# One hybrid decoder layer: output projection and down product turned so that features lie on partitions, the second norm moved behind the MLP

## The chip, the core and the metric

The kernel runs on one core of one Trainium2 chip. A core has TensorE (matmuls of a stationary 128x128 tile with a moving tile of up to 512 columns, into PSUM), VectorE, ScalarE, GpSimd and SP, whose queue issues the DMAs. The metric is device time in microseconds of one execution; lower is better. In the profile TensorE is PE, VectorE is DVE, ScalarE is ACT and GpSimd is POOL.

## The reference

One layer (DEPTH 1) on x of 1024 tokens by 1024 features, all in float32:

```python
merged = gates[:, :, 0] * y_attn + gates[:, :, 1] * y_pool
x = x + jnp.einsum('bsd,de->bse', merged, w_o[l])

h2 = rms_norm(x, norm2_g[l])
u = jnp.square(jax.nn.relu(jnp.einsum('bsd,df->bsf', h2, w_mlp_in[l])))
x = x + jnp.einsum('bsf,fd->bsd', u, w_mlp_out[l])
```

The attention and pooling branches ahead of `merged` are the same in both kernels. The row norm divides each token by the root of its mean square (plus 1e-6) and multiplies each feature by a gain. Since relu squared is homogeneous of second degree, a positive factor r of a token can be left out ahead of the up product and put in as r squared behind the down product.

## The kernel before

**Precision.** Each float32 operand is split into a rounded part (`_hi`, made by ScalarE) and the rest (`_lo`, a subtraction on VectorE, since `_lo = source - _hi`). A product of two such pairs is three matmuls (`passes`): hi by hi, lo by hi (or hi by lo), hi by lo.

**Output projection.** Eight token tiles in the order `ORDER`, two column halves each: 16 PSUM tiles of 128 tokens by 512 features, 24 matmuls each, with the merged activations stationary and `w_o` moving. VectorE adds the residual (`add_res`), SP stores the sum to `res_store`, ScalarE squares and sums the row, GpSimd takes its inverse root, VectorE multiplies by it and by the gain (`h2_norm`), and TensorE turns the row back with eight 128x128 transposes (`h2_transpose`). From the transposed tile ScalarE and VectorE make the hi and lo parts of seven left sides.

**MLP.** Both MLP products go by Winograd's form of Strassen's scheme: 7 products in place of 8. The up product has 16 pairs (`p`) of 256 hidden features; each pair has 7 products P5, P4, P1, P6, P2, P7, P3 of 12 matmuls with 512 columns. Per pair, VectorE makes four sums of the next pair's weights (`t_sums`), five lo parts, four sums of the last results (`u_sums`), three sums out of PSUM (`up_add`), two more lo parts, four more sums; ScalarE rounds, takes relu and square. A PSUM bank is used again by the product eight places on, so the second product of a pair (P4) waits for the sum that frees P5 of the pair before (the third of the last four). The weights come as one 1 MB load per pair into `pair_raw`. Squared activations go to `u_store` in DRAM and come back as `s_raw`.

The down product has 28 products (`n`), 4 chunks of 7, of four tiles with 12 matmuls each. VectorE splits product n+2 while it adds the tiles of n into `acc`, which is first loaded with the residual. In the last chunk GpSimd folds the sums that several quadrants share (`folded`). SP stores most of the output during the last product, and its four tiles (one of them in two halves) as they are done.

**Order.** All queues are written out by hand, each instruction with the semaphores it waits for. What decides the times around the change is the order on VectorE, which the diff shows in full for the projection.

Of the kernel before, what the change touches and what calls it, by code (L numbers as in the profile page):

```python
# [24 lines left out]
F32 = mybir.dt.float32  # L25
# [9 lines left out]
def trunk_layer(nc, x, norm1_g, w_in, b_gate, q_norm_g, k_norm_g, lam_params, subln_g,  # L35
# [26 lines left out]
    y_rows = y.rearrange("b (t p) d -> (b t) p d", p=P)  # L62
# [8 lines left out]
    with ExitStack() as ctx:  # L71
# [79 lines left out]
        ORDER = (4, 0, 5, 1, 6, 2, 7, 3)  # L151
# [4 lines left out]
        res = [at(f"res{i}", kb, [P, D]) for i, kb in enumerate((208, 212, 200))]  # L156
        g2_row = at("g2_row", 144, [P, D])
        a21_f = at("a21_f", 148, [P, QK, P])
        s1_f = at("s1_f", 150, [P, QK, P])
        h2_row = at("h2_row", 152, [P, D])  # L160
        s2_f = at("s2_f", 156, [P, QK, P])
        s34_f = at("s34_f", 158, [P, QK, P])
# [4 lines left out]
        pair_raw = [at(f"pair_raw{i}", 192 + 8 * i, [P, KD, 2 * P]) for i in range(2)]  # L167
# [7 lines left out]
        acc = at("acc", 0, [P, T, D])  # L175
# [18 lines left out]
        res_store = nc.dram_tensor("res_store", [T, P, D], F32, kind="Internal").ap()  # L194
# [13 lines left out]
        N_ROWS = 2 * D // P + GROUPS + 3  # L208
# [4 lines left out]
        small = at("small", 220.25, [P, 128])  # L213
        BG, PS, SG, QG, KG = 0, 2 * D // P, 2 * D // P + GROUPS, 2 * D // P + GROUPS + 1, 2 * D // P + GROUPS + 2
# [26 lines left out]
        def sem(name):  # L241
# [53 lines left out]
        (m_hi, m_split, wo_full, res_ready, r_squared, r_mean, r_inv, h2_ready, h2T_full, h2_hi, h2_f,  # L295
         h2_lo) = (sem(n) for n in (
             "m_hi", "m_split", "wo_full", "res_ready", "r_squared", "r_mean", "r_inv", "h2_ready", "h2T_full",
             "h2_hi", "h2_f", "h2_lo"))
# [3 lines left out]
        o_f, d_hi, d_lo, d_tile, d_added, v_moved, folded, y_ready = (sem(n) for n in (  # L302
            "o_f", "d_hi", "d_lo", "d_tile", "d_added", "v_moved", "folded", "y_ready"))
# [217 lines left out]
        def count_hi(s):  # L521

            return 8 * (s // 2) + 3 * (s % 2)

        def count_f(s):

            return 4 * (s // 2) + s % 2

        def count_lo(s):

            return 7 * (s // 2) + 2 * (s % 2)
# [3 lines left out]

        def b_quarter(p, q):

            return pair_raw[p % 2][(slice(None),) + QUARTER[q]]

        def wo_leaves(eng, p, i):  # L540

            left = i // 2 + 1
            if left == 4:
                eng.wait_ge(wo_full, 2 * T - 1 + p)
            else:
                eng.wait_ge(wo_left, 3 * p + left)
# [2231 lines left out]
```

## Time and profile before

| | |
|---|---|
| time, median of 3 runs | 1241.32 us (1241.32 to 1242.48) |
| profiled execution | 1241.36 us, span 1239.5 us |
| TensorE busy | 1228.6 us, 99% of the span |
| VectorE busy | 945.4 us, 76% |
| ScalarE busy | 563.9 us, 45% |
| GpSimd busy | 139.2 us, 11% |
| granted TensorE clock | 1.00 in every stretch |
| DMA | 173.95 MB, 140 GB/s mean |

The span is the time from the first to the last recorded instruction; the profiled execution's own time holds 1.9 us more. Busy TensorE is the union of matmul intervals, which overlap: a matmul of 512 columns is recorded with 389 ns, but the next starts 227 ns after it. In a timeline a row is `start us, us, engine line instruction out<-in xcount`, and in brackets the idle time ahead of it with what ended it; rows merged with xN are N instructions in a row.

### The profile page before, as it was taken

What the parts mean: (1) busy time and instruction counts of PE and PEld (TensorE: products, weight loads), DVE (VectorE), ACT (ScalarE), POOL (GpSimd) and SP (SyncE); (2) the same over time, 40 slices, a digit from 0 to 9 for tenths busy, and PEclk for the clock granted to TensorE, in tenths of its full rate; (3) what the DMA queues carried; (4) which work ended last, traced back from release to release, by engine and by line L of the source; (5) the groups of instructions that cost most, each with busy time, mean ns of one, the idle gap of its engine ahead of it and who ended that gap; (6) DMA issues with size and microseconds to landing.
All of it is one profiled execution on the core that took longest, in us unless ns stands there. A gap on an engine that the chain in (4) does not pass through costs nothing.

```text
span 1239.5 us, 16100 instructions
## 1 busy us (share of the span) xinstructions
PE 1228.6 (99%) x5822; PEld 1014.1 (82%) x5822; DVE 945.4 (76%) x1334; ACT 563.9 (45%) x971; POOL 139.2 (11%) x188
## 2 busy tenths in 40 slices
PE   8999999999999999999999999999999999999999
PEld 6878888887878888888888888888888888888887
DVE  6857876788887597845678867777769988879764
ACT  7546666665644323312345544535545333333330
POOL 1122233224100040000000000000000000000035
PEclk9999999999999999999999999999999999999999
DMA  9201211023564556422214354353479544262223
GB/s 368 78 17 35 64 40 35 19 60 95 175 235 159 184 172 221 169 86 85 102 60 162 133 173 161 129 178 139 150 263 367 210 157 152 100 237 102 102 100 138
DMA packets 111662, 173.95 MB, mean 140 GB/s; under 512 B 6240, under 2 KB 56288, under 8 KB 111584
## 3 DMA queue, kind: packets, MB, share of 16 engines
q1 hardware_dynamic: 111440, 172.92, 39.9%
q8 instruction: 47, 0.77, 0.3%
q14 instruction: 31, 0.25, 0.1%
q10 hardware_dynamic: 144, 0.00, 0.0%
HBM read 122.57 MB, written 50.33 MB: 139 GB/s over the span
## 4 chain that ended last, share of the span: by engine, by line
PE 88%; DVE 6%; ACT 3%; issue 2%; DMA 1%; SPq 0%; POOL 0%; ACTq 0%; DVEq 0%; POOLq 0%
PE bank L2337 79%; PE bank L2512 2%; PE bank L2467 2%; PE bank L2446 2%; PE bank L2404 1%; DMA x_tile<-in_x 1%; DVE c L2237 1%; DVE pair_lo L2131 1%; PE bank L2395 1%; DVE slot_lo L1532 1%; PE bank L2661 1%; DVE small L1622 1%; ACT prob L1102 0%; DVE gate_w_f L1882 0%; ACT slot_hi L1037 0%
## 5 line engine op out<-in xcount | busy, mean ns | idle before, releaser
L2337 PE MATMUL bank<-o_hi,s_lo 128*128 128x512 f32 (+1 forms) x452 | 175.0, 387 | 0.0
L2337 PE MATMUL bank<-o_hi,s_hi 128*128 128x512 f32 (+1 forms) x452 | 175.0, 387 | 0.0
L2237 DVE TENSOR_TENSOR c<-bank,c 128x512 f32<-128x512 f32 x112 | 75.7, 689 | 34.5 <-PE bank L2337 32.9
L2337 PE MATMUL bank<-featT_hi,pair_hi 128*128 128x512 f32 x256 | 99.8, 390 | 0.8 <-DVE c L2237 0.8
L2337 PE MATMUL bank<-o_lo,s_hi 128*128 128x512 f32 (+1 forms) x260 | 100.3, 386 | 0.0
L2337 PE MATMUL bank<-featT_lo,pair_hi 128*128 128x512 f32 x256 | 99.6, 389 | 0.0
L2337 PE MATMUL bank<-featT_hi,pair_lo 128*128 128x512 f32 x256 | 99.6, 389 | 0.0
L2337 PEld LDWEIGHTS bank<-o_hi,s_lo 128*128 128x128 f32 x452 | 84.9, 188 | 17.3
L2337 PEld LDWEIGHTS bank<-o_hi,s_hi 128*128 128x128 f32 x452 | 84.9, 188 | 17.2
L1500 ACT ACTIVATE s_hi<-s_raw 128x2048 fp32r<-128x2048 f32 x28 | 53.7, 1917 | 95.5 <-DMA s_raw<-u_store 95.5
L1476 ACT ACTIVATE c<-c 128x512 f32<-128x512 f32 x64 | 40.0, 625 | 118.9 <-DVE c L2237 118.9
L2181 DVE TENSOR_TENSOR s_lo<-s_raw,s_hi 128x2048 fp32r<-128x2048 f32 x28 | 65.7, 2348 | 21.8 <-ACT s_hi L1500 21.8
L2337 PE MATMUL bank<-slot_hi,featT_hi 128*128 128x512 f32 x192 | 78.2, 407 | 0.0
L2337 PE MATMUL bank<-slot_lo,featT_hi 128*128 128x512 f32 x192 | 75.1, 391 | 0.0
L2337 PE MATMUL bank<-slot_hi,featT_lo 128*128 128x512 f32 x192 | 74.8, 389 | 0.0
L2337 PE MATMUL bank<-comb_hi,pair_hi 128*128 128x512 f32 x192 | 74.7, 389 | 0.0
L2337 PE MATMUL bank<-comb_hi,pair_lo 128*128 128x512 f32 x192 | 74.7, 389 | 0.0
L2337 PE MATMUL bank<-o_t_lo,s_hi 128*128 128x512 f32 x192 | 74.7, 389 | 0.0
L2337 PE MATMUL bank<-comb_lo,pair_hi 128*128 128x512 f32 x192 | 74.7, 389 | 0.0
L962 POOL TENSOR_SCALAR small<-small 128x1 f32<-128x1 f32 (+2 forms) x58 | 26.1, 450 | 387.4 <-ACT h_row L1462 169.3
L1021 POOL TENSOR_TENSOR p_acc<-p_acc,shared 128x512 f32<-128x512 f32 x4 | 5.2, 1299 | 570.1 <-DVE shared L2295 570.1
L2131 DVE TENSOR_TENSOR pair_lo<-pair_f,pair_hi 128x512 fp32r<-128x512 f32 x64 | 42.8, 688 | 29.8 <-ACT pair_hi L1450 28.8
(270 smaller groups left out, 3135.8 us busy)
## 6 DMA issues: line engine op xcount, KB each, us to landing
s_raw<-u_store SPq DMA_DIRECT2D x28, 1024.0 KB, 5.6
pair_raw<-in_w_mlp_in SPq DMA_DIRECT2D x16, 1024.0 KB, 5.7
u_store<-s_tile SPq DMA_DIRECT2D x64, 256.0 KB, 2.1
o_raw<-in_w_mlp_out SPq DMA_DIRECT2D x16, 1024.0 KB, 8.0
u_store<-u_tile SPq DMA_DIRECT2D x48, 256.0 KB, 2.3
gate_store<-out_tile SPq DMA_DIRECT2D x32, 256.0 KB, 2.1
gate_raw<-in_w_in SPq DMA_DIRECT2D x8, 1024.0 KB, 5.3
front<-in_v_and_high SPq DMA_DIRECT2D x8, 512.0 KB, 7.8
```

The source lines that it names most:

```text
L962: pool.tensor_scalar(ms, ss, 1.0 / n_mean, EPS, ALU.mult, ALU.add).then_inc(mean_sem, 1)
L1476: nc.scalar.activation(c[:], c[:], ACT.Relu).then_inc(relu_done, 1)
L1500: nc.scalar.activation(s_hi[n % 3][:], s_raw[n % 3][:], ACT.Copy).then_inc(d_hi, 1)
L1532: nc.vector.tensor_tensor(slot[1][:, 0:width], raw[r][:, 0:width], slot[0][:, 0:width], ALU.subtract).then_inc(w_ready, 1)
L1622: nc.vector.tensor_reduce(neg_max[u % 2][:, c:c + 1], score_view(u, c), AX.X, ALU.max, negate=True).then_inc(max_ready, 1)
L2131: nc.vector.tensor_tensor(pair_lo[par][:, i], src, pair_hi[par][:, i], ALU.subtract).then_inc(t_ready, 1)
L2181: nc.vector.tensor_tensor(s_lo[n % 3][:], s_raw[n % 3][:], s_hi[n % 3][:], ALU.subtract).then_inc(d_lo, 1)
L2237: nc.vector.tensor_tensor(out[:], psum, other[:], ALU.add).then_inc(up_sum, 1)
L2337: mm = nc.tensor.matmul(out, a, b, start=start and i == 0, stop=stop and i == len(steps) - 1, skip_group_check=onto)
L2446: mm = nc.tensor.matmul(bank[:, 2 * c + p0 // 512 if t >= 4 else 2 * j + c, 0:p1 - p0], a, b, start=i == 0, stop=i == 2)
L2467: mm = nc.tensor.matmul(*m, start=k == 0 and i == 0, stop=k == t and i == 1)
L2512: mm = nc.tensor.matmul(bank[:, v_bank(t), :], featT[a][:, k, columns(t)], v_w[b][:, k, :], start=k == 0 and i == 0, stop=k == KD - 1 and ...
```

## The change

Both products change places of stationary and moving operand, so their results have features on partitions and tokens along the row. The parts:

- Output projection: 16 tiles of 128 features by 512 tokens, first the high token half, then the low one. The residual comes from the transposed copies of x that the kernel gets already. No transposes.
- Instead of the normalised row, ScalarE multiplies the residual by the gain (`gain`) into `z_high` and `z_low`, and VectorE builds the sides from these.
- Mean square: ScalarE squares each tile in place (`square`), GpSimd adds the 8 tiles of a half into `square_sum`, and one fp32 matmul with ones per half (`token_squares`) sums over partitions and spreads the result; VectorE makes `mean` from it (`token_mean`).
- Pair loop: in pairs 1 to 8 SP loads two tiles of `res_store`, VectorE multiplies them by the mean (`scale_res`), SP stores them back. In pairs 9 and 10 VectorE takes a reciprocal of each mean (`mean_inverse`).
- Down product: since the residual was multiplied by the mean, the whole sum is multiplied by the inverse mean at the end: `out_scale` on 12 half tiles of `acc` in the last products and 4 (token half low, first features) earlier, `scale_last_s` on the source of the last product. The output leaves turned and the host turns it back.
- Pair 1's first two products no longer run ahead of pair 0's.

```diff
@@ SP
-            for s in range(T):
-                sp.wait_ge(res_ready, 2 * s + 2)
-                sp.dma_start(res_store[ORDER[s]], res[s % 3][:]).then_inc(res_out[s % 3], 16)
...
+            for n in range(OUTS):
+                store_res(n)
+                if 0 < n < OUTS - 2:
+                    sp.wait_ge(square_added, n)
+                    load_res(n + 2)
...
+                if 1 <= p <= KD:
+                    load_plain(2 * p - 2)
+                    load_plain(2 * p - 1)
...
+                if 1 <= p <= KD:
+                    store_scaled(2 * p - 2)
+                    store_scaled(2 * p - 1)
...
             for t in range(QN):
-                sp.wait_ge(d_added, 4 * (DOWN - 2) + t + 1)
-                sp.dma_start(y_rows[t][:, HALVES[1]], acc[:, t, HALVES[1]]).then_inc(y_out, 16)
-                sp.wait_ge(folded, 3 * QN + t + 1)
-                sp.dma_start(y_rows[QN + t], acc[:, QN + t, :]).then_inc(y_out, 16)
+                sp.wait_ge(out_scaled, QN + 2 * t + 1)
+                sp.dma_start(y[t][:, HIGH], acc[:, t, HIGH]).then_inc(y_out, 16)
+            for t in range(QN):
+                sp.wait_ge(out_scaled, 3 * QN + t + 1)
+                sp.dma_start(y[QN + t], acc[:, QN + t, :]).then_inc(y_out, 16)
+                if t % 2 == 1:
+                    store_last(t // 2)
@@ GpSimd
-            for s in range(T):
-                x_inverse(s, s, r_squared, r_mean, r_inv)
+            for n in range(OUTS):
+                total = square_sum[out_half(n)]
+                pool.wait_ge(squared, n + 1)
+                if n % KD == 0:
+                    pool.tensor_copy(total[:], res[n % 3][:]).then_inc(square_added, 1)
+                else:
+                    pool.wait_ge(square_added, n)
+                    pool.tensor_tensor(total[:], total[:], res[n % 3][:], ALU.add).then_inc(square_added, 1)
@@ ScalarE
+            for n in range(KD, OUTS):
+                j, second = divmod(n - KD, 2)
+                if n == OUTS - 2:
+                    for i in (P5, P4, P1):
+                        t_split_hi(0, i)
+                gain(n)
+                square(n - 1)
+                if n < KD + QK:
+                    bottom_hi(n - KD)
+                if second:
+                    fourth_hi(j)
+                else:
+                    difference_hi(j)
+                if n == OUTS - 2:
+                    top_hi(0)
+                    t_split_hi(0, P6)
+            top_hi(1)
+            t_split_hi(0, P2)
+            square(OUTS - 1)
+            t_split_hi(0, P7)
+            t_split_hi(0, P3)
@@ VectorE
+            add_res(KD + 4)
+            difference_sums(2)
+            bottom_lo(3)
+            comb_lo("s4", 1)
+            add_res(KD + 5)
+            fourth_sum(2)
+            comb_lo("s3", 2)
+            comb_lo("s2", 2)
+            for k in range(4):
+                t_sum(0, k)
+            add_res(KD + 6)
+            difference_sums(3)
+            comb_lo("s4", 2)
+            for i in (P5, P4, P1):
+                t_split_lo(0, i)
+            top_lo(0)
+            add_res(KD + 7)
+            t_split_lo(0, P6)
+            fourth_sum(3)
+            comb_lo("s2", 3)
+            token_mean(1)
+            top_lo(1)
+            t_split_lo(0, P2)
+            comb_lo("s3", 3)
+            t_split_lo(0, P7)
+            comb_lo("s4", 3)
+            t_split_lo(0, P3)
...
                 up_add(3, c11, p2, c11)
                 if more:
                     t_split_lo(p + 1, 5)
                     t_split_lo(p + 1, 6)
+                if p == 0:
+                    token_mean(0)
+                elif p <= KD:
+                    scale_res(2 * p - 2)
+                    scale_res(2 * p - 1)
+                elif p < KD + 3:
+                    mean_inverse(p - KD - 1)
...
+                if n == DOWN - 2:
+                    for t in range(2):
+                        out_scale(t, 1, folded, 2 * QN + t + 1)
+                        out_scale(QN + t, 0, d_added, 4 * n + t + 1)
                 down_add(n, 2)
                 down_add(n, 3)
...
+            for t in range(QN):
+                out_scale(QN + t, 1, folded, 3 * QN + t + 1)
+                if t % 2 == 1:
+                    last_add(t // 2)
@@ TensorE
-                    mm = passes(bank[:, n % 4, :], [(cut(featT, ALL, k, cols), cut(w, ALL, k % 2))],
-                                start=k == 0, stop=k == KD - 1)
+                    mm = passes(bank[:, n % 4, :], [(cut(w, ALL, k % 2, slice(d % 4 * P, (d % 4 + 1) * P)),
+                                                     cut(featT, ALL, k, HALVES[half]))], start=k == 0, stop=k == KD - 1)
...
+            def token_squares(half):
+
+                pe.wait_ge(zeroed, 5)
+                pe.wait_ge(square_added, (OUTS, KD)[half])
+                nc.tensor.matmul(bank[:, SQUARES_BANK[half], :], square_ones[:], square_sum[half][:], start=True,
+                                 stop=True).then_inc(squares_full, 1)
...
+                elif p == 0 and i == P7:
+                    pe.wait_ge(mean_ready, 1)
+                elif p == 1 and i == P5:
+                    pe.wait_ge(mean_ready, 2)
```

## Rows read from the trace of the kernel before

**Rows 1.** The page, busy time of each engine.

```profile
PE 1228.6 (99%) x5822; PEld 1014.1 (82%) x5822; DVE 945.4 (76%) x1334; ACT 563.9 (45%) x971; POOL 139.2 (11%) x188
```

**Rows 2.** Timeline of TensorE around transposes: start us, us, instruction.

```profile
562.48 1.03 PE L2661 MATMUL bank<-ident,h_row 128*128 128x128 f32 x8
563.27 0.48 PE L2337 MATMUL bank<-more_hi,featT_hi 128*128 128x512 f32 x1
...
574.25 1.04 PE L2661 MATMUL bank<-ident,h_row 128*128 128x128 f32 x8
```

**Rows 3.** Timeline of TensorE at the second spread matmul of the first stage.

```profile
35.00 1.02 PE L2526 MATMUL bank<-diagonals,ones 128*128 128x512 f32 x2
...
36.79 1.09 PE L2512 MATMUL bank<-v_w_hi,featT_lo 128*128 128x512 f32 x4
```

**Rows 4.** Timeline of TensorE at its two waits in the up products.

```profile
650.74 0.47 PE L2337 MATMUL bank<-featT_hi,pair_hi 128*128 128x512 f32 x1 [0.15 <-DVE c L2237]
...
667.99 0.47 PE L2337 MATMUL bank<-featT_hi,pair_hi 128*128 128x512 f32 x1 [0.65 <-DVE c L2237]
```

**Rows 5.** Timeline of VectorE in the last 40 us.

```profile
1200.79 3.35 DVE L2181 TENSOR_TENSOR s_lo<-s_raw,s_hi 128x2048 fp32r<-128x2048 f32 x1 [1.39 <-ACT s_hi L1500]
1204.06 1.27 DVE L2295 TENSOR_TENSOR shared<-shared,bank 128x512 f32<-128x512 f32 x2
...
1231.35 0.69 DVE L2302 TENSOR_TENSOR acc<-acc,bank 128x512 f32<-128x512 f32 x1 [2.03 <-PE bank L2337]
1234.07 0.69 DVE L2302 TENSOR_TENSOR acc<-acc,bank 128x512 f32<-128x512 f32 x1 [2.03 <-PE bank L2337]
...
1236.94 0.42 DVE L2302 TENSOR_TENSOR acc<-acc,bank 128x256 f32<-128x256 f32 x1 [1.01 <-PE bank L2337]
```

**Rows 6.** Timeline of GpSimd in the same stretch.

```profile
1200.68 1.30 POOL L1021 TENSOR_TENSOR p_acc<-p_acc,shared 128x512 f32<-128x512 f32 x1
1201.93 3.37 POOL L1022 TENSOR_TENSOR acc<-acc,shared 128x512 f32<-128x512 f32 x1
```

**Rows 7.** Timeline of VectorE in one turn of the pair loop.

```profile
780.82 0.68 DVE L2118 TENSOR_TENSOR pair_f<-pair_raw 128x512 f32<-128x512 f32 x1
...
793.43 0.69 DVE L2237 TENSOR_TENSOR c<-bank,c 128x512 f32<-128x512 f32 x1 [1.25 <-PE bank L2337]
796.00 0.69 DVE L2131 TENSOR_TENSOR pair_lo<-pair_f,pair_hi 128x512 fp32r<-128x512 f32 x1 [1.88 <-ACT pair_hi L1450]
796.61 0.69 DVE L2131 TENSOR_TENSOR pair_lo<-pair_raw,pair_hi 128x512 fp32r<-128x512 f32 x1
797.21 2.73 DVE L2237 TENSOR_TENSOR c<-bank,c 128x512 f32<-128x512 f32 x4
799.86 0.68 DVE L2118 TENSOR_TENSOR pair_f<-pair_raw 128x512 f32<-128x512 f32 x1
```

**Rows 8.** Groups of VectorE instructions: count, busy us, mean ns, idle before.

```profile
L1532 DVE TENSOR_TENSOR slot_lo<-raw,slot_hi 128x1024 fp32r<-128x1024 f32 x12 | 14.5, 1222 | 1.8 <-ACT slot_hi L1037 1.5
...
L1628 DVE RECIPROCAL small<-small 128x2 f32<-128x2 f32 x32 | 5.3, 164 | 8.4 <-ACT prob L1102 8.4
```

**Rows 9.** Timeline of ScalarE in three stretches.

```profile
615.65 1.06 ACT L1462 ACTIVATE h_row<-res 128x1024 f32<-128x1024 f32 x1 [1.36 <-DVE res L2050]
...
783.19 1.14 ACT L1450 ACTIVATE pair_hi<-pair_f 128x512 fp32r<-128x512 f32 x2
...
1209.71 1.92 ACT L1500 ACTIVATE s_hi<-s_raw 128x2048 fp32r<-128x2048 f32 x1 [3.65 <-DMA s_raw<-u_store]
```

**Rows 10.** Timeline of SP's DMA queue in the turn of rows 7.

```profile
790.26 0.46 SPq L818 DMA_DIRECT2D pair_raw<-in_w_mlp_in  x1
```

**Rows 11.** DMA view: GB/s by half microsecond, 785 to 805; issue to landing.

```profile
GB/s 0 0 0 0 0 0 78 381 377 381 381 389 279 274 248 266 375 352 387 387 164 0 152 365 8 0 0 0 0 0 0 0 33 12 365 143 4 0 0 0
...
pair_raw<-in_w_mlp_in SPq DMA_DIRECT2D x16, 1024.0 KB, 5.7
...
out_y<-acc SPq DMA_DIRECT2D x2, 128.0 KB, 1.7
```

More of the change, by code:

```diff
@@ L1438, in t_split_hi, with top_hi @@
+            def top_hi(second):
+                for i in range(2):
+                    two = slice(2 * i, 2 * i + 2)
+                    if second:
+                        act.wait_ge(wo_full, OUTS)
+                    else:
+                        act.wait_ge(wo_left, 5)
+                    nc.scalar.activation(featT[0][:, QK * second + 2 * i:QK * second + 2 * i + 2, LOW], z_low[:, two, second],
+                                         ACT.Copy).then_inc(side_hi2, 1)
             def t_split_hi(p, i):
@@ L1504, in _ @@
                 if more:
-                    for i in range(2 if p == 0 else 0, 5):
+                    for i in range(5):
                         t_split_hi(p + 1, i)
@@ new lines, in comb_lo, with top_lo @@
+            def comb_lo(name, j):
+                pair, plain = {"s2": (comb2, comb2_f), "s3": (comb3, comb3_f), "s4": (comb4, comb4_f)}[name]
+                dve.wait_ge(side_hi2, SIDE_HI[name, j])
+                if name == "s2":
+                    dve.wait_ge(side_sum2, SIDE_SUM["s4", j])
+                nc.vector.tensor_tensor(pair[1][:, j], plain[:, j], pair[0][:, j], ALU.subtract).then_inc(side_lo2, 1)
+            def top_lo(second):
+                for i in range(2):
+                    places = slice(QK * second + 2 * i, QK * second + 2 * i + 2)
+                    dve.wait_ge(side_hi2, SIDE_HI[("a11", "a12")[second], i])
+                    nc.vector.tensor_tensor(featT[1][:, places, LOW], z_low[:, 2 * i:2 * i + 2, second],
+                                            featT[0][:, places, LOW], ALU.subtract).then_inc(side_lo2, 1)
@@ L2215, in _ @@
-            for i in (P7, P3):
-                t_split_lo(0, i)
+            for n in range(KD):
+                add_res(n)
+            add_res(KD)
+            bottom_sum(0)
+            difference_sums(0)
+            add_res(KD + 1)
+            bottom_sum(1)
+            fourth_sum(0)
+            bottom_lo(0)
+            comb_lo("s3", 0)
+            comb_lo("s2", 0)
+            add_res(KD + 2)
+            bottom_sum(2)
+            difference_sums(1)
+            bottom_lo(1)
+            comb_lo("s4", 0)
@@ L2220, in _ @@
                 p5, p4, p1, p6, p2, p7, p3 = (bank[:, product_bank(p, i), :] for i in range(7))
-                if p == 0:
-                    t_sum(1, 3)
-                    for i in range(2, 5):
-                        t_split_lo(1, i)
-                elif more:
+                if more:
                     t_sums(p + 1)
```

466 lines of the change are left out of this document (224 added, 242 removed).

## The prediction

> **What bounds the kernel now.** I read the page's busy shares first: TensorE is busy 99% of the span [rows 1]. Then its timeline, for gaps: behind the output projection only VectorE's sums hold it, 0.15 and 0.65 us in two places [rows 4]. TensorE issues a 128x512 matmul each 0.227 us (12 of them, one tile of 512 columns, 2.72: the last adds follow at that distance [rows 5]), and between the gaps it never rests. So time leaves only if TensorE issues less or waits less, and it returns wherever another engine is late. The other engines have little room in three places: the change from output projection to MLP, the loop over MLP pairs, and the end. The profiled execution took 1241.36 us with a span of 1239.5, so 1.9 lie around it; the median of the three runs is 1241.32, the same. About 0.2% (2.5 us) is what a measurement of this kernel can tell from no change.
>
> **TensorE's own work.** The turned products keep number and shape: 384 matmuls of 512 columns in the output projection, and the same in up and down products. Before, 48 matmuls take 10.88, yet from one group of eight transposes to the next are 11.77 [rows 2]: a group costs 0.89 with the slower start behind it. Eight groups go: **-7.1**. Two matmuls of plain fp32 against a tile of ones come (the token sums of squares). The spread matmul of the first stage has that shape and type, two passes each; from its start to the second group behind it are 1.79, of which four ordinary matmuls are 0.91, so one costs 0.88 [rows 3]: **+1.8**. The two waits of before in pairs 0 and 1 are of the old order and go. Their rows give 0.15 and 0.65 idle [rows 4]; the matmul ahead is recorded 0.16 past the next normal start, and the one behind starts its successor 0.08 late (0.47 or 0.48 recorded for 0.39), so together 0.31 + 0.81 + 0.16: **-1.3**.
>
> **GpSimd's adds and VectorE.** New on GpSimd are 16 adds of 128x512 from SBUF, one per projection tile (each 5.44 us). The trace shows what that does [rows 5, 6]: VectorE's subtraction of two 128x2048 SBUF tiles (2.29 by the growth of 0.53 per 512 in rows 8) takes 3.35 when issued while GpSimd's add runs, and the add behind it takes 3.37 instead of 1.30. The starts and ends fit turns: VectorE waits until the add is over (about 1201.95), then GpSimd until VectorE is (1204.1). VectorE's two adds with a PSUM operand at 1204.06 run beside GpSimd unhindered, 1.27 for both. So each new add costs VectorE 1.25 where its next operation has two SBUF operands. The Trainium skill (GPSIMD Engine Reference, Specifications) says that GpSimd's SBUF interfaces are shared with VectorE and contend with VectorE instructions that have two SBUF inputs; by that rule, too, the adds are not free, and the trace agrees.
>
> **From projection to MLP.** I walk through VectorE's new order; zero is the moment at which TensorE is through with the last projection tile. An operation of 512 elements costs 0.60 start to start [rows 7], one of 1024 1.13 (0.60 and the 0.53 between durations of 1.222 [rows 8] and 0.69), the PSUM ones the same. ScalarE takes 0.52 per 512 and about 1.0 per 1024 [rows 9], and its result is usable 0.66 after its start. Tiles 9 to 12 give VectorE 6 or 7 operations each (4.2) plus 1.25 plus 0.2 to 0.4 of waits for ScalarE's gain: 5.1 to 5.9 per 5.44, so it enters tile 13 on time, at -10.5. Tile 13: 8 operations 4.8, GpSimd 1.25, waits for own results and for the gain 1.15: done at -3.3. Tile 14: 7 operations 4.2, two wide 2.3, GpSimd 1.25, wait for the gain 0.75: done at 5.2. The first weight split in it is ready at 1.8, so TensorE starts the MLP 1.8 late. Tile 15: 10 operations 6.0, two wide 2.3, two GpSimd adds 2.5, waits 0.15: 16.1. The split for the fifth product is ready at 13.8, wanted at 12.7: 1.1 more. Then pair 1: four sums 2.8 and five splits 3.0 to 21.9; from the first PSUM sum to the sixth split, through ScalarE's relu, square and two roundings, 3.9 (two sums of 0.67 and 793.43 to 796.00 [rows 7]) to 25.8; two splits 1.2 to 27.0; the mean of the low half 0.7: 27.7. Pair 1's first product waits for that mean, because it writes the bank that held the squares. TensorE, undisturbed, would be there at 7 x 2.72 + 0.88 = 19.9. All its waits there come to **+7.8**, and three restarts **+0.2**. Without the turns with GpSimd the mean ends at 23.2 and the waits are 3.3; that is the lower bound. The work it queues behind (sums of pair 0, splits) is late together, but not later than TensorE needs it.
>
> **The pair loop.** In pairs 1 to 8 SP issues, behind the weight load, two loads of plain residual (256 KB each); VectorE scales both between its seventh split and its fourth sum. Before, one turn of VectorE starts at 780.82, SP issues the weight load at 790.26, VectorE's fourth sum starts at 797.21 and the next turn at 799.86 [rows 7, 10]. The load lands 5.7 after issue, the queue moving up to 390 GB/s around it [rows 11]; 0.52 MB more take 1.35, so the second plain tile lands 7.05 after issue: 9.45 + 7.05 + 0.6 (scaling) + 2.65 (four sums) = 19.75 for one turn. TensorE's pair is 7 x 2.72 = 19.05. Pair 1 starts with no slack (its turn ends at 27.7 + 2.6 + 19.75 less 0.6, TensorE wants the bank at 27.7 + 21.8), so pairs 2 to 8 lose 0.7 each: **+5.0**. If the tiles land 0.7 earlier it is nothing; 0.7 later, 10.
>
> Two reciprocals of 128x512 follow, in pairs 9 and 10. The only ones of before have two elements, 164 ns [rows 8], which says nothing of the rate. Lower bound: as any operation of 512, 0.69, hidden in VectorE's idle time of the pair, 1.25 at one place alone [rows 7]; upper: some 4 us, as 2 us of slack are all there is (the third of the four sums from 797.21 ends at 799.3 and frees the bank; TensorE's second product of that pair starts at 801.4, which is 667.99 [rows 4] and 7 pairs of 19.05). 
>
> **The end.** Before, 3.15 MB of the output go out as soon as the next-to-last product's adds are done, under the last product's matmuls; the end is the last add at 1236.94, 0.42 long [rows 5], and its 128 KB (1.7 to landing [rows 11]). After, the output must first be multiplied by the inverse mean: one 128x2048 multiply before the last product's split, and 12 of 128x512 from two SBUF tiles in the last two products, in turns with GpSimd's eight folds. The source lands at 1209.7, when ScalarE starts on it [rows 9]; behind GpSimd's add the wide multiply ends at 1213.4 and, through ScalarE's 1.92, the last split at 1218.1 (wanted when the last product starts, three tiles before the add at 1231.35: about 1225.7). Then, placing adds at TensorE's 2.72 and taking turns of 0.6 and 1.25, eight multiplies end at 1232.9, and the four that complete the full rows at 1233.5, 1234.1, 1235.3 and 1235.9. Those release 2.1 MB and the last adds 1.05 MB. From 1233.6 on, 3.15 MB at 390 GB/s [rows 11] are 8.1, and 1.7 for issue and landing: 1243.4, against 1239.5: **+3.9**. Without turns the first such row goes at 1230.1 and the end is as before: 0. The front stages change nothing on a path: the eight gain columns ride on a load that lands long before.
>
> **Sum.** -7.1 + 1.8 - 1.3 + 7.8 + 0.2 + 5.0 + 3.9 = +10.3 on 1239.5, 1249.8; with 1.9 around it **1251.7 us**.
>
> **Rivals.** (1) *The residual loads are in time.* Turns with GpSimd and the burst at the end cost as above, the loop nothing: 1246.7. For it: the landing estimate decides by 0.7. Against: pair 1 starts without slack, so a late tile is late for TensorE at once. (2) *The removed transposes win.* VectorE is never held by GpSimd's short adds because they fall on its PSUM operations or idle time: -7.1 + 1.8 - 1.3 + 3.3 + 0.2 = -3.1, 1238.2. It decides where the mean ends before 26.3 (19.9 and the 6.4 that the other terms give back) with loop and end at nothing; against it stand the turns above [rows 5, 6]. (3) *The reciprocals are slow,* as the Trainium skill's repeat count has it: two stalls of about 2 in pairs 9 and 10, 1255.7. (4) *Gain and loss cancel:* half of the turns, loop in time, a small burst: within 2.5 of before.
>
> **Numbers.** Forecast 0.42 (own range 1248.5 to 1254.5), rival 1 0.2, rival 3 0.15, rival 2 0.12, rival 4 0.11. The range reaches down to 1240 (part of rival 4 in, rival 2 out) and up to 1257 (rival 3 with a landing a little later). Faster: rival 2, 0.12. Same: rival 4, 0.11 and a shred of rival 1: 0.12. Slower: 0.76.
>
> **What would show it.** No transpose rows, and between two projection tiles 10.88 per 48 matmuls. TensorE gaps of some 1.8, 1.1 and 4.9 us before pair 1's first product, with VectorE's mean as releaser. VectorE operations of 128x512 with two SBUF operands lasting up to 1.9 in the projection. TensorE gaps of about 0.7 at each pair from 2 to 8, and VectorE waiting for the plain residual's DMA. A RECIPROCAL of 128x512 near 0.7. DMA at its full rate for the last 8 us. The prediction is wrong if VectorE reaches the mean by 23, or if the last full rows leave before 1230 of the old time scale.

## The result and the profile after

The changed kernel takes **1264.31 us** (median, 1264.04 to 1265.66, 4 runs) against 1241.76 for the kernel before on the same chip: ratio 1.0183, 95% interval 1.0166 to 1.0201. It is slower, as forecast, but by 22.5 us and not by 10, and outside the range (1240 to 1257).

The page of the changed kernel, to be set beside [rows 1]:

```profile
span 1262.5 us, 16093 instructions
...
PE 1230.9 (98%) x5762; PEld 1012.1 (80%) x5762; DVE 976.7 (77%) x1359; ACT 572.0 (45%) x979; POOL 156.7 (12%) x189
...
PE   8999999999999999999989999999999999999997
...
PEclk9999999999999999999989999999999999999999
```

VectorE has 31 us more work, GpSimd 17.5. TensorE issues 60 instructions fewer and is still recorded 2.3 us busier. The clock row, full in every slice before, has one slice at 8: the one from 631 to 663 us, in the first two pairs of the MLP. The same stretches by window (stretch, its length, TensorE busy with the number of matmuls, granted clock as a share, DMA share, GB/s):

```profile
618.00:628.00 10.00, 8.16 (x30) 0.83 0.45 150
628.00:644.00 16.00, 15.26 (x66) 1.00 0.21 66
644.00:656.00 12.00, 8.69 (x27) 0.72 0.12 45
656.00:688.00 32.00, 32.00 (x143) 1.00 0.61 205
688.00:700.00 12.00, 9.71 (x37) 0.86 0.30 112
700.00:880.00 180.00, 171.42 (x750) 1.00 0.53 180
```

**Where the 23 us are.** The output projection starts at the same time in both profiles (its first matmul at 531.64 before, 531.51 after). From there to the start of the last matmul it is 704.98 before (1236.62) and 723.39 after (1254.90): 18.4 more. Behind that start the span ends 2.9 us later before and 7.6 after: 4.7 more. TensorE's timeline at the start of the MLP shows the first part of it, two waits and what follows each:

```profile
619.23 0.39 PE L2480 MATMUL bank<-featT_lo,more_hi 128*128 128x512 f32 x1
621.45 0.47 PE L2480 MATMUL bank<-featT_hi,pair_hi 128*128 128x512 f32 x1 [1.83 <-DVE comb_lo L2163]
...
622.21 0.63 PE L2480 MATMUL bank<-featT_hi,pair_hi 128*128 128x512 f32 x1
622.64 0.63 PE L2480 MATMUL bank<-featT_hi,pair_lo 128*128 128x512 f32 x1
...
642.87 0.39 PE L2480 MATMUL bank<-comb_lo,pair_hi 128*128 128x512 f32 x1
647.31 0.77 PE L2480 MATMUL bank<-featT_hi,pair_hi 128*128 128x512 f32 x1 [4.05 <-DVE mean L2178]
647.88 0.63 PE L2480 MATMUL bank<-featT_hi,pair_lo 128*128 128x512 f32 x1
...
652.97 0.40 PE L2480 MATMUL bank<-featT_hi,pair_lo 128*128 128x512 f32 x1
653.21 0.39 PE L2480 MATMUL bank<-featT_lo,pair_hi 128*128 128x512 f32 x1
```

The reader is to look at the distance between starts, not at the bracket alone. Before the wait of 4.05 us a matmul follows the last by 0.227; behind it 13 in a row follow by 0.43, which is the 1.2 GHz level of the clock in place of 2.4 (the granted clock of this stretch is 0.72 in the window row). Only at 652.97 is the pace back. A wait of 4.05 us thus costs 4.2 between starts and 2.6 more behind it. The stretch at 622.21 is the same, 8 matmuls, 1.6 us; a third begins at 694.18, with 8 more and 1.6 us.

The pair loop, one turn of VectorE, with the queue of SP (SPq) below it, to be set beside [rows 7, 10]:

```profile
734.60 0.68 DVE L2208 TENSOR_TENSOR pair_f<-pair_raw 128x512 f32<-128x512 f32 x1
...
748.62 0.69 DVE L2221 TENSOR_TENSOR pair_lo<-pair_raw,pair_hi 128x512 fp32r<-128x512 f32 x1
751.05 1.33 DVE L2185 TENSOR_TENSOR scaled_res<-scaled_res,mean 128x512 f32<-128x512 f32 x2 [1.75 <-DMA scaled_res<-res_store]
752.29 2.73 DVE L2338 TENSOR_TENSOR c<-bank,c 128x512 f32<-128x512 f32 x4
754.95 0.68 DVE L2208 TENSOR_TENSOR pair_f<-pair_raw 128x512 f32<-128x512 f32 x1
```

```profile
744.03 0.46 SPq L855 DMA_DIRECT2D pair_raw<-in_w_mlp_in  x1
744.53 1.46 SPq L846 DMA_DIRECT2D scaled_res<-res_store  x2
```

VectorE stands 1.75 us for the plain residual, loaded behind the weights. The second of the two tiles can hold it too, as two pairs later:

```profile
793.48 0.69 DVE L2185 TENSOR_TENSOR scaled_res<-scaled_res,mean 128x512 f32<-128x512 f32 x1 [0.29 <-DMA scaled_res<-res_store]
```

Its turn lasts 20.35 us (734.60 to 754.95), the next 20.94, TensorE's pair 19.05. TensorE pays at the second product of a pair: the first of these gaps, an ordinary one and the first of the two that belong to the reciprocals are

```profile
693.29 0.47 PE L2480 MATMUL bank<-featT_hi,pair_hi 128*128 128x512 f32 x1 [2.29 <-DVE c L2338]
...
734.23 0.47 PE L2480 MATMUL bank<-featT_hi,pair_hi 128*128 128x512 f32 x1 [1.00 <-DVE c L2338]
...
837.22 0.47 PE L2480 MATMUL bank<-featT_hi,pair_hi 128*128 128x512 f32 x1 [1.16 <-DVE c L2338]
```

Six such gaps from 693 to 817 (start to start less 0.227: 2.45, 1.16, 1.18, 1.80, 1.72, 1.20) are 9.5 us, with their restarts (0.08 each, as in the two waits of before) 10.0. Two more of 1.31 at 837 and 858 belong to the reciprocals (2.8 with restarts). The groups of VectorE show what one costs, beside the small one that was all that the trace before had [rows 8]:

```profile
L2191 DVE RECIPROCAL mean<-mean 128x512 f32<-128x512 f32 x2 | 6.7, 3347 | 0.0
...
L1707 DVE RECIPROCAL small<-small 128x2 f32<-128x2 f32 x32 | 5.2, 164 | 8.4 <-ACT prob L1154 8.4
```

In the sum: -6.6 (transposes, ones-matmuls and the two old waits, the forecast values, which no experiment took apart), +2.1 and +4.3 (the two waits), +5.8 (three stretches at 1.2 GHz), +10.0 (pair loop), +2.8 (reciprocals): 18.4, which is the measured difference. One reservation: 1.6 of the 5.8, at 622, fills time in which TensorE would otherwise have waited for a split and for the mean; without it those waits are longer. In experiment 2's profile, where the clock stayed up there, the three waits are 1.83, 0.72 and 4.63.

The end, first VectorE, then the DMA rate in forty equal slices from 1240 to the end of the span:

```profile
1239.95 6.07 DVE L2418 TENSOR_TENSOR acc<-acc,mean 128x512 f32<-128x512 f32 x4
...
1253.77 1.28 DVE L2418 TENSOR_TENSOR acc<-acc,mean 128x512 f32<-128x512 f32 x2
1254.98 1.93 DVE L2426 TENSOR_TENSOR acc<-acc,bank 128x512 f32<-128x512 f32 x4
```

```profile
GB/s 0 0 0 317 139 0 0 0 0 360 96 0 0 0 0 0 0 228 228 0 0 228 228 214 406 399 406 392 371 428 420 392 392 388 381 388 337 159 0 0
```

The last add ends at 1256.9, and the transfers go on at some 390 GB/s until about 1261. Four multiplies in 6.07 are 1.5 each (two undisturbed ones at 1253.77 take 1.28 together), beside six folds of GpSimd that fill the time from 1234.54 to 1245.47. The first full row is multiplied at 1252.65, 2.3 before the start of the last matmul; the forecast had 3.1.

### The profile page after: what moved, and what is told of

Same layout as the page of the kernel before. It is cut to its first block, busy times and chain, and to the rows that moved or that the text cites. A ratio compares the mean times of both kernels' runs of the same rounds, so it can differ in the third digit from the quotient of the medians.

```text
span 1262.5 us, 16093 instructions
## 1 busy us (share of the span) xinstructions
PE 1230.9 (98%) x5762; PEld 1012.1 (80%) x5762; DVE 976.7 (77%) x1359; ACT 572.0 (45%) x979; POOL 156.7 (12%) x189
## 4 chain that ended last, share of the span: by engine, by line
PE 74%; DVE 13%; DMA 5%; ACT 3%; issue 3%; SPq 1%; POOL 0%; DVEq 0%; ACTq 0%; POOLq 0%
PE bank L2480 65%; DMA scaled_res<-res_store 4%; PE bank L2655 2%; DVE pair_lo L2221 2%; PE bank L2610 2%; PE bank L2589 2%; DVE c L2338 2%; DVE pair_f L2208 1%; PE bank L2547 1%; DMA x_tile<-in_x 1%; SPq L899 1%; DVE scaled_res L2185 1%; DVE small L1701 1%; DVE slot_lo L1611 1%; ACT pair_hi L1521 1%
## 5 line engine op out<-in xcount | busy, mean ns | idle before, releaser
L2480 PE MATMUL bank<-s_lo,o_hi 128*128 128x512 f32 (+1 forms) x452 | 175.0, 387 | 0.0
L2480 PE MATMUL bank<-s_hi,o_hi 128*128 128x512 f32 (+1 forms) x452 | 175.0, 387 | 0.0
L2480 PE MATMUL bank<-s_hi,o_lo 128*128 128x512 f32 (+1 forms) x260 | 100.3, 386 | 0.0
L2480 PEld LDWEIGHTS bank<-s_hi,o_hi 128*128 128x128 f32 x452 | 84.9, 188 | 17.3
L2480 PEld LDWEIGHTS bank<-s_lo,o_hi 128*128 128x128 f32 x452 | 84.9, 188 | 17.1
L2480 PE MATMUL bank<-s_hi,o_t_lo 128*128 128x512 f32 x192 | 74.7, 389 | 0.0
L2480 PEld LDWEIGHTS bank<-featT_hi,pair_hi 128*128 128x128 f32 x256 | 49.4, 193 | 30.8 <-issue 14.0
L2480 PEld LDWEIGHTS bank<-featT_lo,pair_hi 128*128 128x128 f32 x256 | 49.4, 193 | 10.7
L2480 PEld LDWEIGHTS bank<-featT_hi,pair_lo 128*128 128x128 f32 x256 | 49.7, 194 | 10.2
L2480 PEld LDWEIGHTS bank<-s_hi,o_lo 128*128 128x128 f32 x260 | 48.8, 188 | 9.9
```

What stands on the lines that cost most here:

```text
L2480: mm = nc.tensor.matmul(out, a, b, start=start and i == 0, stop=stop and i == len(steps) - 1, skip_group_check=onto)
```

## The experiments

Each starts from the changed kernel unless it says otherwise, and each ratio is against the kernel before, run on the same chip (medians of before 1241.81 to 1242.29). A gain is the changed kernel's 1264.31 less the experiment's median. The kernel before differs by up to 0.5 us between these chips; taken against it on each chip, the gains come out up to 0.5 larger, and none is good to better than that. The first, profiled execution of a series is up to 2.9 us above its median, so times are medians and the profiles serve for single rows. The front stages end up to 2.3 us apart from run to run; rows are therefore read from the start of the projection or from the end of it.

**1. GpSimd's adds cut to one column.** The sums of squares leave out 511 of 512 columns in seven tiles of eight.

```diff
-                    pool.tensor_tensor(total[:], total[:], res[n % 3][:], ALU.add).then_inc(square_added, 1)
+                    pool.tensor_tensor(total[:, 0:1], total[:, 0:1], res[n % 3][:, 0:1], ALU.add).then_inc(square_added, 1)
```

> Starts from the changed kernel. GpSimd's 14 adds of squares handle one column of 512, so the token sums of squares leave out the other 511 columns of seven tiles in eight; everything else is unchanged. Theory (turns between GpSimd's adds and VectorE's operations with two SBUF operands make VectorE late): VectorE's operations of 1.1 to 1.8 us beside the adds go back to 0.69, the mean of the low half ends about 23.2 us behind the end of the projection in place of 27.7, the gap of 2.0 us before the first MLP product and the half-clock stretch behind it (1.6) go, and the waits at pair 1 fall from some 6 us to 3 or less, with a half-clock stretch behind them only if the wait stays above 2 us: 5 to 9 us faster than the changed kernel, 1255 to 1259. Rival (VectorE is late by its own work, the adds are beside the point): the mean within 1 us of its old place, under 2 us gained.

Measured 1260.57 (ratio 1.0149, 1.0134 to 1.0165), 3.7 less than the changed kernel. The VectorE operation beside GpSimd's add in projection tile 9, in the changed kernel (VectorE, then GpSimd) and here:

```profile
582.95 1.68 DVE L2149 TENSOR_TENSOR comb_f<-comb_f,z_high 128x512 f32<-128x512 f32 x1
...
646.48 0.68 DVE L2178 TENSOR_SCALAR mean<-bank 128x512 f32<-128x512 f32 x1
```

```profile
582.78 1.29 POOL L1068 TENSOR_TENSOR square_sum<-square_sum,res 128x512 f32<-128x512 f32 x1 [4.14 <-ACT res L1476]
```

```profile
583.92 0.69 DVE L2149 TENSOR_TENSOR comb_f<-comb_f,z_high 128x512 f32<-128x512 f32 x1
...
643.51 0.68 DVE L2178 TENSOR_SCALAR mean<-bank 128x512 f32<-128x512 f32 x1
```

1.68 becomes 0.69. The projection's last matmul starts at 620.21 here and at 619.23 above, so the mean ends 23.8 us behind the end of the projection in place of 27.7. The turns are shown, and so is the lower bound of the prediction (23.2). The wait before the first product went. But TensorE still waits 3.80 us for the mean (3 or less was expected): the mean is 3.9 earlier, and so is TensorE by nearly as much, without the first wait (2.1) and the stretch at 1.2 GHz behind it (1.6). The clock still drops behind the mean (0.86 from 644 to 656). From the first projection matmul to the last of all the profile is 5.2 shorter, and the end takes 0.4 of that back (8.0 behind the last matmul in place of 7.6). The remaining wait is why the gain is below the expected 5 to 9.

**2. Plain residual loads one pair earlier.**

```diff
-                if 1 <= p <= KD:
-                    load_plain(2 * p - 2)
-                    load_plain(2 * p - 1)
...
                 store_u(D4, p, u_tile[2])
+                if p < KD:
+                    load_plain(2 * p)
+                    load_plain(2 * p + 1)
```

> Starts from the changed kernel. The two plain residual loads of pair p+1 are issued one pair earlier, behind the first store of squared activations of pair p, and not behind the weight load; same bytes. Theory (the plain tiles land too late for VectorE's scaling, which delays the sum that frees the bank of the next pair's second product): the six TensorE gaps of 1.2 to 2.5 us in pairs 2 to 8 go, with the half-clock stretch of 1.6 us at 693: 9 to 12 us faster than the changed kernel, 1252 to 1255. Rival 1 (VectorE's own work, 1.2 us more a pair by the scalings, makes the turn too long): the gaps stay near 1 us each, under 4 us gained. Rival 2 (0.5 MB more a pair fill the queue wherever they are issued): the wait moves to the weight load or the stores, under 4 us gained.

Measured 1252.97 (1.0089, 1.0074 to 1.0104): 11.3 less, the largest single gain. All six gaps are gone, and the third stretch at 1.2 GHz with them; the windows of this kernel from 688 on:

```profile
688.00:700.00 12.00, 12.00 (x55) 1.00 0.48 168
700.00:880.00 180.00, 177.69 (x783) 1.00 0.55 188
```

The loads now take 3.5 us to landing at the median, 6.5 behind the weights:

```profile
scaled_res<-res_store SPq DMA_DIRECT2D x16, 256.0 KB, 3.5
```

VectorE's own work in a turn is the same, so rival 1 is out; the bytes are the same, so rival 2 is out. What is left of the 180 us are the reciprocals' 2.3.

**3. The reciprocals in thirds,** in pairs 9 to 14.

```diff
-                nc.vector.reciprocal(mean[half][:], mean[half][:]).then_inc(inverse_ready, 1)
+                half, third = divmod(part, 3)
+                cols = slice(*((0, 176), (176, 344), (344, 512))[third])
+                done = nc.vector.reciprocal(mean[half][:, cols], mean[half][:, cols])
...
-                elif p < KD + 3:
+                elif p < KD + 7:
```

> Starts from the changed kernel. Each 128x512 reciprocal of 3.35 us is done in three column parts, one in each of pairs 9 to 14. Theory (one reciprocal exceeds the slack of VectorE in a pair by about 1.3): both gaps of 1.31 us at 837 and 858 go, 2.6 to 3.0 us faster, 1261.5. The parts would last 1.1 us each if the cost is by element. Rival (the cost is per instruction, the parts last as long as the whole): six gaps of 1.3, 5 us slower.

Measured 1262.32 (1.0161, 1.0144 to 1.0178): 2.0 less (2.6 in the profiles, from the first projection matmul to the last of all). Both gaps at 837 and 858 are gone, and the parts cost by their columns:

```profile
L2193 DVE RECIPROCAL mean<-mean 128x168 f32<-128x168 f32 x4 | 4.8, 1196 | 0.0
L2193 DVE RECIPROCAL mean<-mean 128x176 f32<-128x176 f32 x2 | 2.5, 1248 | 0.0
```

Between 168 and 512 columns the time grows by 2151 ns, 6.25 ns a column; an add of this shape grows by 0.53 us per 512 [rows 7, 8], 1.0 ns a column.

**4. The mean ahead of pair 0's sums.**

```diff
-                if p == 0:
-                    token_mean(0)
-                elif p <= KD:
+                if 0 < p <= KD:
...
+                if p == 0:
+                    token_mean(0)
                 dve.wait_ge(first_copied, p + 1)
                 dve.wait_ge(p_done, turn(p, P6))
```

> Starts from the changed kernel. VectorE makes the mean of the low half ahead of pair 0's last seven operations (sums out of PSUM, two splits) and not behind them. Theory A (VectorE as a whole is late; the sums that it postpones are wanted next, since the third of them frees the bank of the second product of pair 1): TensorE's wait for the mean goes, most of it comes back at the next bank, 1 to 3.5 us gained. Rival B (only the mean's own place in the order makes TensorE wait): the 4.2 us of wait and the half-clock stretch behind it all go, 4.5 to 7 us gained.

Measured 1263.16 (1.0175, 1.016 to 1.0191): 1.2 less, which the runs alone hardly tell from nothing (1263.14 to 1265.89 against 1264.04 to 1265.66). The profile decides, for theory A: TensorE no longer waits for the mean but, one product later, for the sum that frees that bank, just as long:

```profile
650.30 0.76 PE L2480 MATMUL bank<-featT_hi,pair_hi 128*128 128x512 f32 x1 [3.98 <-DVE c L2338]
```

So the wait is VectorE's lateness, whatever instruction ends it.

**5. Low halves of the full rows stored early.**

```diff
                 sp.dma_start(y[t][:, HIGH], acc[:, t, HIGH]).then_inc(y_out, 16)
+                sp.wait_ge(out_scaled, QN + 2 * t + 2)
+                sp.dma_start(y[QN + t][:, LOW], acc[:, QN + t, LOW]).then_inc(y_out, 16)
             for t in range(QN):
                 sp.wait_ge(out_scaled, 3 * QN + t + 1)
-                sp.dma_start(y[QN + t], acc[:, QN + t, :]).then_inc(y_out, 16)
+                sp.dma_start(y[QN + t][:, HIGH], acc[:, QN + t, HIGH]).then_inc(y_out, 16)
```

> Starts from the changed kernel. The low token halves of the four full output rows are stored as soon as they are multiplied, and only the high halves with the last four multiplies: about 1 MB less in the burst at the end. Theory (the end is set by 3.15 MB that become ready together and leave at about 400 GB/s): the tail behind the last matmul falls from 7.6 us by 1 MB at 400 GB/s, 2.0 to 2.6 us faster, near 1262. Rival (issue and landing of the last store alone set the end, or VectorE's last multiplies do): under 0.7 us gained.

Measured 1261.18 (1.0156, 1.0139 to 1.0172): 3.1 less. The last matmul of its profile starts at 1255.83 and the span is 1261.5: the tail is 5.7 and not 7.6, 1.9 less. That is about the size expected (2.0 to 2.6). Another 1.0 stands ahead of the last matmul (722.43 from the first projection matmul, 723.39 in the changed kernel), where this edit changes nothing: in this profile the first wait is followed by no stretch at 1.2 GHz.

**6. A product done twice, to fill TensorE's wait.**

```diff
+                if (p, i) == (0, P3):
+                    passes(bank[:, product_bank(p, i), :], operands)
                 passes(bank[:, product_bank(p, i), :], operands).then_inc(p_done, 1)
```

> Starts from the changed kernel. TensorE does the last product of pair 0 twice into the same bank, 12 more matmuls of 512 columns (2.72 us), ahead of its wait for the mean of the low half. Theory (the wait lasts until VectorE's mean whatever TensorE does, and the half clock behind it comes from TensorE's rest): the wait falls from 4.05 to about 1.3 us, the 13 matmuls at 0.43 us behind it go at 0.227, and the kernel with more work is 1.5 to 3 us faster, near 1262. Rival (the slow stretch comes from the matmuls behind it, their operands or ports, not from the rest): the stretch stays, no change or up to 2.7 us slower by the second product being late for VectorE's sums.

Measured 1261.29 (1.016, 1.0145 to 1.0175): with 12 more matmuls it is 3.0 us faster. The matmuls behind the wait:

```profile
645.96 0.39 PE L2480 MATMUL bank<-comb_lo,pair_hi 128*128 128x512 f32 x1
648.27 0.47 PE L2480 MATMUL bank<-featT_hi,pair_hi 128*128 128x512 f32 x1 [1.92 <-DVE mean L2178]
648.58 0.40 PE L2480 MATMUL bank<-featT_hi,pair_lo 128*128 128x512 f32 x1
648.81 0.39 PE L2480 MATMUL bank<-featT_lo,pair_hi 128*128 128x512 f32 x1
```

The same matmuls with the same operands go at 0.23 at once, and the granted clock from 644 to 656 is 1.00. The mean still ends 27.7 us behind the end of the projection (647.44 + 0.68 against 620.41), so it is VectorE's time and not TensorE's that sets it. What slowed these matmuls was TensorE's rest before them. It is no accident of one profile: the mean granted clock of all four executions is 0.997 or 0.998 here and 0.992 to 0.995 in the changed kernel.

**7. Edits 2, 3, 4 and 5 together.**

> Starts from the changed kernel. Residual loads one pair earlier, reciprocals in three parts, mean of the low half ahead of pair 0's sums, low halves stored early, all four together. If the four losses are separate and add up: 11 + 2.8 + 2.3 + 2.3, about 18 us faster than the changed kernel, near 1246, still 4 to 5 us behind the kernel before (the turns with GpSimd, the fp32 matmuls and the rest of the burst stay). If they hide each other, 1250 or more. If the four are worth more than the rows say, 1240 or less.

Measured 1247.99 (1.0048, 1.0033 to 1.0063): 16.3 less, 2 short of the 1246 expected, where the four alone sum to 11.3 + 2.0 + 1.2 + 3.1 = 17.6. The losses are separate for the most part. From 660 us to the end of the down product no gap of TensorE is above 0.5 us; what is left is the start of the MLP (1.83, 0.74 and 3.95 of wait, the clock at 0.77 behind the last).

**8. Pair 0's sums ahead of five splits.**

```diff
-                    for i in range(5):
+                    for i in range(2 if p == 0 else 5):
                         t_split_lo(p + 1, i)
...
-                if more:
+                if more and p > 0:
                     t_split_lo(p + 1, 5)
                     t_split_lo(p + 1, 6)
...
                 up_add(7, c12, p3, c12)
+                if p == 0:
+                    for i in range(2, 7):
+                        t_split_lo(1, i)
```

> Starts from the changed kernel. VectorE does pair 0's seven sums out of PSUM and the mean behind only two of pair 1's weight splits; the other five splits, which TensorE needs 2.7 us apart, come behind the sums. Same instructions. Theory (the wait of 4 us at pair 1 is five splits of 0.6 us, 3.0, and 1.9 us of idle time for ScalarE's rounding, both done ahead of need): the mean and the third of the last four sums come about 4 us earlier, the wait of 4.05 us falls below 1 us, the half clock behind it goes (2.6), 4 to 7 us faster than the changed kernel, near 1259. Pair 2's first wait (2.3 us) may shrink too. Rival (VectorE's total work up to there counts, whatever the order): the wait moves to a split, under 2 us gained.

Measured 1262.04 (1.0162, 1.0146 to 1.0178), only 2.3 less. The wait of 4.05 for the mean is gone but for 0.3, yet two others stand in the pairs behind it:

```profile
668.54 0.47 PE L2483 MATMUL bank<-featT_hi,pair_hi 128*128 128x512 f32 x1 [3.20 <-DVE c L2338]
...
691.12 0.76 PE L2483 MATMUL bank<-featT_hi,pair_hi 128*128 128x512 f32 x1 [3.28 <-DVE c L2338]
```

Neither my theory nor the rival had this. VectorE's rows ahead of these two sums name what is late:

```profile
665.02 1.32 DVE L2185 TENSOR_TENSOR scaled_res<-scaled_res,mean 128x512 f32<-128x512 f32 x2 [2.53 <-DMA scaled_res<-res_store]
...
687.60 1.33 DVE L2185 TENSOR_TENSOR scaled_res<-scaled_res,mean 128x512 f32<-128x512 f32 x2 [4.01 <-DMA scaled_res<-res_store]
```

In the changed kernel VectorE did not wait for this DMA in pair 1, and 3.02 in pair 2. Both engines come there sooner, and the residual loads, covered before by the wait for the mean, now hold them. If that is the reason, the same edit must be worth its full amount where the loads are early, which experiment 10 tests.

**9. The low half's squares summed by TensorE** in place of GpSimd.

```diff
+            def take_squares(n):
+                pe.wait_ge(squared, n + 1)
+                nc.tensor.matmul(bank[:, SQUARES_BANK[0], :], square_ones[:].bitcast(F32R), res_r[n % 3][:],
+                                 start=n == KD, stop=n == OUTS - 1).then_inc(square_taken, 1)
...
+                    if n >= KD + 2 and k == 5:
+                        take_squares(n - 2)
```

> Starts from the changed kernel. The squares of the low half's eight tiles (rounded to fp32r by ScalarE) are summed by TensorE, one 128x512 matmul each, in place of GpSimd's eight adds and one fp32 matmul. Theory: VectorE loses no turns in tiles 8 to 15, as with one-column adds, the mean ends 3.5 to 4 us earlier relative to the projection's end, and TensorE pays 8 x 0.227 for 0.88, 0.9 us more: 2 to 3.5 us faster than the changed kernel, near 1261.5. Rival (the fp32r matmul switches weights and types and costs more than 0.3 us each, or waits for ScalarE's square): gaps at the eight places, no gain.

Measured 1259.61 (1.0149, 1.0135 to 1.0163): 4.7 less, more than the 2 to 3.5 expected. The wait before the first product is gone as in experiment 1; the wait for the mean (4.44) stays for the same reason as there.

**10. Edits 2, 3, 5 and 8 together.**

> The changed kernel with four edits: residual loads one pair earlier, reciprocals in thirds, low halves stored early, pair 0's sums ahead of five splits; GpSimd's adds stay. If the losses are separate: 11 + 2.5 + 2.8 + 5.5 = 22 us faster than the changed kernel, 1242 to 1244, level with the kernel before. If the order of sums is worth no more than the mean moved alone: 1247.

Measured 1242.21 (1.0005, 0.9996 to 1.0014; 10 runs): no different from the kernel before. Taking the gains of edits 2, 3 and 5 alone from 1264.31 gives 1247.9; edit 8 is worth 5.7 here (4.6 with all gains taken against the kernel before on each chip, 4.9 from the profiles) and was worth 2.3 alone. Of the two waits of 3.2 and 3.3 that it met alone, the second is gone and the first is down to

```profile
668.24 0.47 PE L2489 MATMUL bank<-featT_hi,pair_hi 128*128 128x512 f32 x1 [0.58 <-DVE c L2344]
```

The reason given under 8 holds.

**11. Edits 2, 3, 5, 8 and 9 together.**

> The four edits together with the low half's squares summed by TensorE. If all named losses are the whole of it: TensorE's own work is 6.6 less than before, 0.9 more for the fp32r matmuls, the tail 2.6 longer, no wait above 0.3 us elsewhere: 3 us under the kernel before, 1238 to 1240. If a wait remains that I did not name (pair 0's split of the fifth product, pair 2's first sums): 1241 to 1244.

Measured **1240.15** (1239.18 to 1242.04, 11 runs) against 1241.83: ratio 0.9986, 0.9978 to 0.9995. It beats the changed kernel by 24 us and the kernel before by 1.7, barely, at the upper edge of what was expected (1238 to 1240). Its windows, to be compared with those of the changed kernel above:

```profile
618.00:628.00 10.00, 9.31 (x41) 1.00 0.43 141
644.00:656.00 12.00, 11.70 (x52) 1.00 0.27 89
688.00:700.00 12.00, 12.00 (x55) 1.00 0.77 254
700.00:880.00 180.00, 180.00 (x796) 1.00 0.53 180
```

From its first projection matmul (533.60) to its last of all (1235.53) are 701.9, 3.1 less than before; the tail is 4.7 against 2.9.

## Why the prediction was wrong

The direction, the places and most mechanisms were right. The sum was 10.3 and the rows of after have 23.1; the 12.8 between them are a cost of rests that was put at next to nothing (4.2), the pair loop (5.0), the reciprocals (2.8) and the end (0.8).

- **TensorE's own work, -7.1 + 1.8 - 1.3.** Consistent: with it, the rows of after add up to the measured 18.4. A token-squares matmul costs 0.87 (0.88 said). No experiment took the three terms apart.
- **GpSimd and VectorE in turns.** Right, shown by experiment 1. The mean ends 27.7 us behind the end of the projection, the forecast value, and the first MLP product is 2.0 late where 1.8 was said. The experiment without turns gives 23.8 for the forecast 23.2.
- **From projection to MLP, +7.8 and +0.2.** The waits are as forecast (6.2 us, and the 1.6 at 622 that fill the rest; where the clock stays up, in experiment 2, they are 7.7). The step that failed is the price of a wait: I counted a restart as 0.1, from waits of 0.15 and 0.65 us [rows 4]. Behind waits of 2 to 4 us the clock fell to 1.2 GHz and the matmuls went at 0.43 in place of 0.227: 2.6 behind the mean, 1.6 in the loop, 4.2 not forecast. Experiment 6 shows the cause. That no row of before had such a wait was a reason to keep the cost open, and I didn't give it a bound. The Trainium skill (TensorE: Matmul & The Clock Gate, "Part 1") says that a hardware block sets TensorE's clock to half or full rate by how busy it has been; the rows agree, and I should have weighed it as a case that speaks against the change.
- **The pair loop, +5.0.** The mechanism was right (experiment 2), the size was 10.0. The turn was to last 19.75 and lasts 20.35 and 20.94. The term that failed is the landing. SP issues the weights 9.43 into the turn (734.60 to 744.03), as forecast. But the weight load lands 6.2 us later and not 5.7, the second plain tile 1.3 behind it, as said, and so 7.6 after the issue and not 7.05; from its scaling (751.68) on, the rest is as forecast. Over the seven turns in which these loads hold VectorE the weights land after 6.2 to 6.9 and the second tile after 7.6 to 8.3, 0.8 later than forecast on average, which makes about the missing 5 us. My own "0.7 later, 10" had the value. The 5.7 came from turns in which no load followed the weights; in experiment 2, where none does again, it is 5.8. That the loads behind slow the one ahead is the likely reason and was not tested by itself.
- **The reciprocals, 0.** Wrong: 3.35 us each, 1.31 past the slack, 2.8 in all (gone in experiment 3, 2.0 by medians). I took the lower bound "nearest in shape" though the operation was another; the nearest row in operation (two elements, 164 ns) could not decide. Rival 3 had the mechanism. The Trainium skill (VectorE: DVE Perf Modes, "First, the fixed hardware budget") has the repeat count of 8, from which I had estimated 4.3 us; the trace shows 3.35, 22% under that estimate and five times the 0.69 that I took.
- **The end, +3.9.** Right in kind, 4.7 measured: the first full row is ready 0.8 later than forecast. The turns of VectorE with the folds and the stores' burst are both there; experiment 5 takes 1.9 of it away by storing a third earlier.
- **The rivals.** Residual loads in time: false. Transposes win: false; experiment 11 had to build its conditions (an early mean, nothing in the loop), and even there the end costs 1.8 more than before. The forecast with rival 3 gives 1255.7; the clock adds 4.2 and the longer loop 5.0 to that, and 1264.3 is then within 1 us.

What stays open: when a rest is followed by 1.2 GHz. Behind the same wait of 1.83 us before the MLP the clock fell in the profiles of the changed kernel and of experiments 3 and 8, and stayed at 2.4 GHz in those of 2, 4, 5, 6, 7 and 10; behind 3.20 in experiment 8 and 2.55 in experiment 1 it stayed up as well. So among waits of 1.8 to 3.2 us the length alone does not decide. The turns at the end (multiplies against folds) were read from rows and not taken away by an experiment.

## What to carry to other kernels

Where TensorE is 99% busy, price a new wait on it twice: the wait itself, and the matmuls at half clock that came behind 16 of the 25 waits of 1.8 us and more that these profiles have behind the projection (2.6 us of delay behind the longest of the changed kernel); filling the wait with useless matmuls was cheaper than resting. When work moves to a loaded engine, the order in which that engine serves its consumers is worth as much as the amount: some seven of the 24 us recovered here came from sums placed before splits that nobody wanted yet and from adds moved off the neighbour that blocks it, eleven from a load issued one turn earlier. And a fix that gains less than its wait was long is not yet refuted: look for the next late thing, mend that, and measure the first again.

## What the runs showed of the hardware

- A RECIPROCAL of 128x512 fp32 on VectorE takes 3347 ns, 6.25 ns a column between 168 and 512 columns, against 0.69 us for an add of that shape.
- TensorE at 1.2 GHz behind a rest: matmuls of 512 columns 0.43 apart, 13 of them behind 4.05 us of wait, 8 behind 1.83 and 8 behind 2.29; none behind waits of 1.0 to 1.7, and none behind some longer ones (3.20 in experiment 8, 2.55 in experiment 1, 1.83 in six of nine profiles).
- A GpSimd add of 128x512 (1.29 us) and a VectorE operation with two SBUF operands exclude each other for the whole instruction: 0.69 became 1.68. VectorE's adds with a PSUM operand kept their 0.67 to 0.69 beside GpSimd's folds, one of 3.37 [rows 5, 6] and the six in a row from 1234.54 on.
- Summing the squares with one fp32r matmul of ones for each tile cost 0.227 us in TensorE's stream where its operand was there; eight replaced a GpSimd copy, seven GpSimd adds and a two-pass fp32 matmul of 0.87.
- A 1 MB load and the loads behind it in SP's queue: with two loads of 256 KB issued behind, the 1 MB landed after 6.2 to 6.9 us and the 256 KB ones 6.5 after their own issue; issued apart from it, 5.8 and 3.5 (medians, experiment 2).
